# The norms' per-token factor moved behind the weight products, and x times norm weight split tile by tile

## The reference

```python
def rmsnorm(x, g):
    xf = x.astype(F32)
    y = xf * lax.rsqrt(jnp.mean(xf * xf, axis=-1, keepdims=True) + EPS)
    return (y * g.astype(F32)).astype(x.dtype)

h = rmsnorm(x, w['norm_mix'][i]);  x = x + mixer(h)
h = rmsnorm(x, w['norm_ffn'][i])
f = (jax.nn.silu(h @ w['ffn_w_gate'][i]) * (h @ w['ffn_w_up'][i])) @ w['ffn_w_down'][i];  x = x + f
```

## Time and profile before

| | |
|---|---|
| median of three runs | 1917.39 us (1916.46 to 1919.80) |
| the profiled execution | 1914.43 us, span 1912.6 us, mean granted TensorE clock 0.978 |
| PE busy | 1816.6 us (95%), 13287 matmuls |
| PE weight load busy | 1751.6 us (92%) |
| POOL busy | 849.4 us (44%) |
| ACT busy | 619.5 us (32%) |
| DVE busy | 592.2 us (31%) |
| DMA | 153.23 MB, mean 80 GB/s |

### The profile page before, as it was taken

How to read it: one execution, slowest core, us unless ns; L and a number is a source line. 1 busy time by engine, 2 the same in 40 slices (tenths; PEclk the granted TensorE clock), 3 DMA queues, 4 the chain that set the end, 5 groups by cost and what they waited for, 6 DMA issues and landing times.

```text
span 1912.6 us, 33665 instructions
## 1 busy us (share of the span) xinstructions
PE 1816.6 (95%) x13287; PEld 1751.6 (92%) x13287; DVE 592.2 (31%) x887; ACT 619.5 (32%) x846; POOL 849.4 (44%) x1061
## 2 busy tenths in 40 slices
PE   6998999997999999999999999999988999999997
PEld 4898989886999999999999999999977999999996
DVE  2545454555211111000453355344534111111002
ACT  3625252523222222113333333424334222222112
POOL 2544444444454544446443344334424445444443
PEclk9999999997999999999999999999988999999998
DMA  5113121211222222223231343134321222322221
GB/s 149 45 34 79 43 78 44 79 34 46 66 81 82 82 79 83 80 83 103 73 117 58 114 128 112 59 117 119 106 64 58 78 87 77 88 77 83 80 83 57
DMA packets 254284, 153.23 MB, mean 80 GB/s; under 512 B 5136, under 2 KB 246549, under 8 KB 254240
## 3 DMA queue, kind: packets, MB, share of 16 engines
q1 hardware_dynamic: 239726, 140.05, 25.4%
q10 hardware_dynamic: 14514, 12.59, 2.0%
HBM read 138.26 MB, written 14.36 MB: 80 GB/s over the span
## 4 chain that ended last, share of the span: by engine, by line
PE 49%; issue 15%; POOL 10%; DVE 3%; ACT 1%; DMA 0%; POOLq 0%; ACTq 0%; DVEq 0%
PE acc L465 40%; POOL w_lo L457 9%; PE acc L485 7%; PE mx L1511 1%; DVE n_xf L587 1%; PE mx L883 1%; PE mx L528 0%; POOL n_ss L565 0%; POOL xn_lo L571 0%; DVE yT L587 0%; DMA out<-y_out 0%; DVE xn_lo L571 0%; POOL kdm L980 0%; DVE y_out L1506 0%; PE mx L524 0%
## 5 line engine op out<-in xcount | busy, mean ns | idle before, releaser
L457 POOL TENSOR_TENSOR w_lo<-raw,w_hi 128x256 fp32r<-128x256 f32 x932 | 712.7, 797 | 941.5 <-ACT w_hi L449 941.5
L465 PE MATMUL acc<-xn_hi,w_hi 128*128 128x288 f32 x2224 | 498.1, 306 | 2.4 <-ACT kb L721 1.3
L465 PE MATMUL acc<-xn_hi,w_lo 128*128 128x288 f32 x2224 | 477.6, 296 | 0.0
L465 PE MATMUL acc<-xn_lo,w_hi 128*128 128x288 f32 x2224 | 476.8, 296 | 0.0
L449 ACT ACTIVATE w_hi<-raw 128x1024 fp32r<-128x1024 f32 (+1 forms) x237 | 247.0, 1043 | 528.9 <-PE acc L465 528.2
L465 PEld LDWEIGHTS acc<-xn_hi,w_hi 128*128 128x128 f32 x2224 | 358.6, 190 | 15.7 <-issue 7.9
L465 PEld LDWEIGHTS acc<-xn_lo,w_hi 128*128 128x128 f32 x2224 | 359.2, 189 | 0.0
L465 PEld LDWEIGHTS acc<-xn_hi,w_lo 128*128 128x128 f32 x2224 | 358.9, 189 | 0.0
L601 DVE TENSOR_TENSOR x<-acc,x 128x576 f32<-128x576 f32 (+1 forms) x112 | 84.7, 756 | 323.1 <-PE acc L465 321.4
L693 DVE TENSOR_TENSOR f_h<-acc,f_g 128x576 f32<-128x576 f32 x44 | 33.3, 758 | 443.8 <-PE acc L465 443.8
L465 PE MATMUL acc<-h_hi,w_hi 128*128 128x288 f32 x704 | 150.9, 295 | 0.0
(11 more groups left out here) (326 smaller groups left out, 2134.8 us busy)
## 6 DMA issues: line engine op xcount, KB each, us to landing
raw<-in_odd_w_in SPq DMA_DIRECT2D x48, 512.0 KB, 3.7
raw<-in_ffn_w_gate SPq DMA_DIRECT2D x44, 512.0 KB, 3.7
raw<-in_ffn_w_up SPq DMA_DIRECT2D x44, 512.0 KB, 3.7
raw<-in_ffn_w_down SPq DMA_DIRECT2D x32, 512.0 KB, 3.7
raw<-in_even_w_in SPq DMA_DIRECT2D x29, 512.0 KB, 4.0
r_s<-in_state_ret SPq DMA_DIRECT2D x8, 1024.0 KB, 5.5
...
```

The lines of the kernel that those rows point to most:

```text
L457: ins = nc.gpsimd.tensor_tensor(w_lo[:, d, piece], raw[:, s, piece], w_hi[:, d, piece].bitcast(F32), ALU.subtract)
L465: ins = nc.tensor.matmul(out, w, mv[:, tokens], start=first and n == 0, stop=last and n == 2)
```

## The change

For norms 1, 2 and 3 the factor n_rs no longer goes into the moving operand. As a tile of x is finished, ACT squares it and rounds x times norm weight into xn_hi (`square_and_scale`), and DVE forms the remainder in one instruction (`late_low`), between its additions to x. Norms 0 and 4 stay as they were. PE starts the first two units of the next part on these tiles: slices 0 to 5 of both, then `norm_sum`, then slices 6 and 7 of both (`late_units`). POOL now adds seven squares in every norm from 1 on.

The factor is applied where products leave the accumulators. In the feed-forward part DVE multiplies the gate product with n_rs (f_g), ACT applies Silu in place, DVE multiplies f_g with n_rs again, and with the second accumulator. In the odd mixer DVE empties values and gates with n_rs as factor, and ACT applies Silu to the gates afterwards, in place; for q and k the rotary tables `co` are multiplied with n_rs once.

Three further moves: the rows of the convolution states are transposed and copied within the last even head, and SP sends them; the waits for outgoing DMAs ahead of the feed-forward loops go from ACT to DVE; and `rows_unit` begins its first slice when the operand's first half is there (`yl0`, `yal`) and waits for the second half at its second slice. f_h is gone (h_lo takes its place) and zi, xi share the memory of n_sq.

```diff
-O_ACT = ("kdt", "v0", "v1", "ot", "osq", "oln", "oinv", "yh0", "yh1")
+O_ACT = ("kdt", "v0", "v1", "gs0", "ot", "gs1", "osq", "oln", "oinv", "yh0", "yh1")
...
+        def late_units(pe, norm, one, other):
+            for a, b in ((0, KT - 2), (KT - 2, KT)):
+                for phase, j in (one, other):
+                    unit(pe, phase, 0, j, a, b, wait_late=norm)
+                if a == 0:
+                    norm_sum(pe, norm)
...
+                    if mb == 0 and k == 1 and low_1:
+                        low_1()
...
-        POOLED = (0, 5, 7, 5, 7)
+        POOLED = (0, 7, 7, 7, 7)
...
+        def gain(k, t):
+            return cols[:, COL_NORM[k] + t:COL_NORM[k] + t + 1]
+        def square_and_scale(act, k, t):
+            square(act, k, t)
+            nc.scalar.activation(xn_hi[:, t, :], x[:, t, :], ACT.Copy, scale=gain(k, t)).then_inc(q_hi, 1)
+        def late_low(dve, k, t):
+            dve.wait_ge(q_hi, k * KT + t + 1)
+            nc.vector.scalar_tensor_tensor(out=xn_lo[:, t, :], in0=x[:, t, :], scalar=gain(k, t),
+                                           in1=xn_hi[:, t, :].bitcast(F32), op0=ALU.mult,
+                                           op1=ALU.subtract).then_inc(q_low, 1)
...
-            with pe.Fori(0, FT // 2) as i:
-                for t in range(2):
-                    unit(pe, up, i, 2 * t, wait_norm=k if t == 0 else None)
-                    unit(pe, up, i, 2 * t + 1)
+            late_units(pe, k, (up, 0), (up, 1))
+            for j in (2, 3):
+                unit(pe, up, 0, j)
+            with pe.Fori(1, FT // 2) as i:
+                for j in range(4):
+                    unit(pe, up, i, j)
             pe.wait_ge(f_lo, (layer + 1) * FT - 1)
             with pe.Fori(0, KT // 2) as i:
...
-                    act.wait_ge(multiplied, plan.summed(up, i, 2 * t))
-                    act.wait_ge(drained[1], plan.drained(up, i, 2 * t + 1))
-                    nc.scalar.activation(f_g[:, :], pair_view(0), ACT.Silu).then_inc(drained[0], 1)
+                    act.wait_ge(drained[0], plan.drained(up, i, 2 * t) + 1)
+                    nc.scalar.activation(f_g[:, :], f_g[:, :], ACT.Silu).then_inc(f_act, 1)
...
+                    dve.wait_ge(multiplied, plan.summed(up, i, 2 * t))
+                    nc.vector.tensor_tensor(f_g[:, :], pair_view(0), n_rs[:, :], ALU.mult).then_inc(drained[0], 1)
+                    dve.wait_ge(f_act, 2 * n - 1)
+                    nc.vector.tensor_tensor(f_g[:, :], f_g[:, :], n_rs[:, :], ALU.mult).then_inc(f_act, 1)
+                    dve.wait_ge(f_act, 2 * n)
                     dve.wait_ge(multiplied, plan.summed(up, i, 2 * t + 1))
-                    dve.wait_ge(drained[0], plan.drained(up, i, 2 * t) + 1)
-                    nc.vector.tensor_tensor(f_h[:, :], pair_view(1), f_g[:, :], ALU.mult).then_inc(drained[1], 1)
+                    value = ff_tile(h_lo, i, t)
+                    nc.vector.tensor_tensor(value.bitcast(F32), pair_view(1), f_g[:, :], ALU.mult)\
...
+            late = norm_next < 4
+            with dve.Fori(0, KT // 2 - 1 if late else KT // 2) as i:
                 for t in range(2):
                     add_to_x(dve, down, i, t, ds(i * 2 + t, 1))
+            if late:
+                for t in range(KT - 2):
+                    late_low(dve, norm_next, t)
+                for t in range(2):
+                    add_to_x(dve, down, KT // 2 - 1, t, KT - 2 + t)
+                    late_low(dve, norm_next, KT - 2 + t)
...
+            def activate_gate(d):
+                emptied(act, phase, i, 2 + d)
+                o_act.done(nc.scalar.activation(gs[:, d, :], gs[:, d, :], ACT.Silu), f"gs{d}")
...
-            evac(3, gs[:, 1, :], ACT.Silu)
+            activate_gate(1)
             load_table(LN_EXP)
             o_dve.wait(act, h, "cen")
             o_act.done(nc.scalar.activation(osq[:, :, :], of[:, :, :], ACT.Square), "osq")
...
+            dve.wait_ge(q_rs, 3)
+            for n in range(2):
+                ins = nc.vector.tensor_tensor(co[:, n, :], co[:, n, :], n_rs[:, :], ALU.mult)
+            ins.then_inc(s_co, 1)
...
+            def values(j):
+                p = plan.pair(phase, j)
+                dve.wait_ge(multiplied, plan.summed(phase, i, j))
+                nc.vector.tensor_tensor(va[:, j, 0:TP], pair_view(p)[:, 0:TP], n_rs[:, 0:TP], ALU.mult)
+                nc.vector.tensor_tensor(spread(va[:, j, TP:]), pairs(pair_view(p)[:, TP:T]), pairs(n_rs[:, TP:T]),
+                                        ALU.mult).then_inc(drained[p], 1)
+            def gate_in(d):
+                p = plan.pair(phase, 2 + d)
+                dve.wait_ge(multiplied, plan.summed(phase, i, 2 + d))
+                nc.vector.tensor_tensor(gs[:, d, :], pair_view(p), n_rs[:, :], ALU.mult).then_inc(drained[p], 1)
...
             step(ins, "cen")
+            gate_in(1)
             o_act.wait(dve, h, "osq")
             step(nc.vector.tensor_tensor(both[:, :], osq[:, 0, :], osq[:, 1, :], ALU.add), "sq_both")
...
                 add_to_x(dve, phase, i, PLAIN[phase] + m, m)
+                if last and m >= 2:
+                    late_low(dve, 3, m - 2)
...
-            o_dve.wait(pe, h, "yl1")
+            o_dve.wait(pe, h, "yl0")
             for j in range(2):
-                rows_unit(pe, phase, i, PLAIN[phase] + j, PLAIN[phase] + 4 * j, oyh, oyl)
+                rows_unit(pe, phase, i, PLAIN[phase] + j, PLAIN[phase] + 4 * j, oyh, oyl,
+                          low_1=(lambda: o_dve.wait(pe, h, "yl1")) if j == 0 else None)
...
+            for n in range(4):
+                sp.wait_ge(rows_copied, n + 1)
+                k = 2 if n == 0 else 3
...
-            squares_while_splitting(act, split_hi, square, 1, EVEN_END)
-            norm_scalar(act, 1)
-            for n in range(4):
...
+            squares_while_splitting(act, split_hi, square_and_scale, 1, EVEN_END)
+            norm_scalar(act, 1, late=True)
             ffn_scalar(act, 0)
...
+                if last and m:
+                    late_low(dve, 1, m - 1)
+            if last:
+                late_low(dve, 1, KT - 1)
...
+            if last:
+                emptied(pe, phase, i, 3)
+                emptied(pe, phase, i, 4)
+                for t in range(4):
+                    ins = nc.tensor.transpose(acc[0:18, 0, 0, t * P:(t + 1) * P], out_a[:, t, :], ident)
+                ins.then_inc(rows_turned, 1)
...
-            e_dve.wait(pe, h, "ybl")
+            e_dve.wait(pe, h, "yal")
+            if last:
+                pe.wait_ge(rows_copied, 4)
+            e_act.wait(pe, h, "yah")
             for j in range(2):
-                rows_unit(pe, phase, i, PLAIN[phase] + j, PLAIN[phase] + 4 * j, yh, yl)
+                rows_unit(pe, phase, i, PLAIN[phase] + j, PLAIN[phase] + 4 * j, yh, yl,
...
-            pe.wait_ge(rows_copied, 4)
-            norm_sum(pe, 1)
             ffn_tensor(pe, 0)
-            norm_sum(pe, 2)
-            two_units(pe, 2, ("odd_kq", 0), ("odd_kq", 1))
+            late_units(pe, 2, ("odd_kq", 0), ("odd_kq", 1))
             with pe.Fori(0, RET_H - 1) as i:
```

131 lines of the change are left out of this document (59 added, 72 removed).

## The result

Changed kernel 1912.98 us median (20 runs, 1908.85 to 1921.78); kernel before beside it 1917.36 us (20 runs, 1913.82 to 1922.48). Ratio 0.9980, 95% interval 0.9970 to 0.9989. It is faster, as forecast, but by 4 us and not by 9.6. A later comparison of the same two gave 1912.27 against 1917.99, ratio 0.9967 (0.9950 to 0.9984). I take 4.4 to 5.7 us as the gain.

The account below looks back on a forecast made before the run. PE was taken to bound the kernel, other engines counting only where PE waits. 4 + 7.8 + 1 + 1.6 - 4.8 = 9.6 us off gave 1904.8, or 1908 on the median's footing; own range 1900 to 1913, with neighbours 1895 to 1917.

Parts of the forecast that it names:

- Boundary 2: Down phase into the odd mixer: U(0) starts at 919.9, before at 928.59; gain 8.7 less 0.9, so 7.8 us.
- the slow stretch: PE at a lowered clock after a gap; 0.9 us taken off at the second boundary for a possible one.
- the rule of blocked ports: Two-SBUF-input VectorE and SBUF-reading GpSimd instructions block each other wholly; some 3 to 5 us less gain in all.
- Odd heads: Second gate's detour over DVE delays unit 5's split: PE waits 1.3, 0.6 returns; net loss 0.7 us, seven heads 4.8.
- Boundary 3: Last odd head into the second up phase: unit 2 at 1474.3, gain 4.75, slow stretches about 3.7; gain 1 us.
- Boundary 1: Last even head into the first up phase: unit 2 at 484.8 for 492.7, 7.9 us less 4 for clock; gain 4.
- Even heads: Output groups start on the first half while PE would wait for yl; three heads win 1.6 us.
- Up and down loops: Feed-forward loops: two more DVE products per pair of units and Silu 0.85 us later, costed at nothing.
- the rival of 1936 us: Up-phase loops: DVE's second f_g product stretches POOL's split, weight 0.7 us late in 40 places, 28 us; chance 0.08.
- gain eaten by the split chain: Unit 5's wait costs 1.6 us or more a head, late_low blocked at boundaries 1 and 3: 1917 us; chance 0.17.
- the full gain of 21 us: Rival: gaps too short or well placed to lower the clock, odd heads cost little; 1896 us, chance 0.2.

Follow-up runs that it names:

- u0_early: Changed kernel with ScalarE splitting U(0)'s weights before it waits for the norm's sum, not behind the inverse root: 1909.96 us against 1917.99 for the kernel before.
- gate_late: Changed kernel with the odd heads' second-gate Silu and table load moved behind the squares and U(5)'s weight split: 1901.92 us against 1917.99 for the kernel before.
- both_lows: Changed kernel with the output groups waiting for both rounding residues again, in even and odd heads: 1913.14 us against 1917.94 for the kernel before.

## Why the prediction was wrong

The direction and the places were right, and the time lies in the range. The size was not: 4.4 to 5.7 us for 9.6. By its own steps:

*Boundary 2: the step that failed most, 5.3 us measured for 7.8.* What failed is the price of POOL's splits beside DVE's new instructions, put at the price of an undisturbed split, and the size of the slow stretch. The text has "n_rs at 915.6, then ACT splits the first head's weight (1.05) and POOL (2.8): 919.8", and from there 8.7 less 0.9. The chain was right and ran as written:

```profile
919.55 0.69 ACT L575 ACTIVATE n_rs<-n_rs 128x576 f32<-128x576 f32 x1
920.14 1.05 ACT L446 ACTIVATE w_hi<-raw 128x1024 fp32r<-128x1024 f32 x1
```

```profile
921.27 3.65 POOL L454 TENSOR_TENSOR w_lo<-raw,w_hi 128x256 fp32r<-128x256 f32 x4 [9.58 <-ACT w_hi L446]
```

Three sizes in it were off. POOL's split took 3.65 us and not 2.80, as DVE multiplied beside it (how, stands under the rule of blocked ports): U(0) began 18.1 us after the down phase's end, for 17.4. That end itself came 1.1 us later, counted from down0's first addition, than before (PE's first slice of the key unit at 906.96, its norm sum before at 902.50, and 3.4 us of offset). DVE's late_low now runs beside POOL there, and PE waits 0.33 and 0.22 us for w_lo, which it didn't; its matmuls shift by the whole 1.1 us at these two stops. The 16 pieces of w_lo in 880:907 have a mean of 938 ns,

```profile
L454 POOL TENSOR_TENSOR w_lo<-raw,w_hi 128x256 fp32r<-128x256 f32 x16 | 14.5, 938 | 2.3 <-ACT w_hi L446 2.3
```

against 739 of 17 in the like stretch before. I had counted that the down phase gives ACT and DVE 17 us a tile and forgot what their work does to POOL's. And the slow stretch behind the gap took 1.7 us, not 0.9 (from U(0)'s start to the first product of rotated queries and keys 8.01 us for 6.34). Together 8.7 - 0.7 - 1.1 - 1.7 = 5.2, measured 5.3. What I should have said is that a split put behind the inverse root is free to move ahead of it: u0_early shows 4.1 us at that one place.

*Odd heads.* "Net 0.7 us, in seven heads: 4.8 us": measured 0.88, 6.2 us. The mechanism was right. In the frame of the head, PE's variance product came 0.17 us later, which I had put at nothing; from there to the kvs product it took 9.68 us for 8.29, that is 1.39 more where I had 1.3 (the row at 1037.31 shows 1.06 of it as a wait); and 0.7 came back at the output groups, for 0.6. gate_late confirms the cause: 0.77 of the 0.88 us goes with the order alone. In the last head PE's wait for the sum of squares grew by 1.5 us (4.08 to 5.57) and that at the output groups fell by 0.8 (3.62 to 2.82), both as forecast.

*Boundary 3.* 1.0 forecast with the last odd head, 0.0 measured. In the heads' frame, which is 4.3 us later than before, unit 0 began at 1452.1, where I had 1452.3. Unit 1 began at 1460.8 for 1460.0: POOL's two splits ahead took 3.30 and 3.28 us for 2.80, and its three additions spanned 5.5 us for 4.3, all with late_lows beside them. Unit 2 began at 1477.2 for 1474.3, 1.9 us earlier than before where I had 4.75. The rest of that difference is a low clock behind unit 1's wait, 1.7 us, and a wait that was 0.5 longer:

```profile
1465.10:1471.10 6.00, 6.00 (x34) 6.00 (x35) 0.00 (x0) 0.00 (x0) 0.00 (x0) 0.72 0.29 87
1481.40:1487.40 6.00, 5.98 (x31) 5.98 (x32) 0.00 (x0) 0.00 (x0) 2.72 (x4) 0.66 0.60 173
```

Behind unit 2 the clock took the remaining 1.9. In all it cost 3.6 us, for 3.7 forecast; the term that failed is mainly POOL's price again.

*Boundary 1.* 4.0 forecast with the last even head. A mark ahead of the early start shows both parts at once, the first copy of oT in that head. Before and after:

```profile
437.17 0.23 DVE L1416 COPY oT<-mx 128x64 f32<-128x64 f32 x1 [2.12 <-PE mx L1511]
```

```profile
444.56 0.23 DVE L1468 COPY oT<-mx 128x64 f32<-128x64 f32 x1 [0.76 <-PE mx L1568]
```

From here to down0's first addition it is 342.45 us before and 338.43 after: 4.0 us won, as forecast (338.5 and 337.0 in the changed kernel's other profiles, 342.3 to 344.6 in those of the kernel before). On this footing unit 0 began at 464.3 for 464.7, unit 1 at 471.7 for 470.5, unit 2 at 486.4 for 484.8, and the two slow stretches cost 1.7 and 2.4 us, for the 4 taken off. The clock differs in that head too: from the copy to the first output addition PE had 0.50 before and 0.83 after, so a part of the 4.0 may be luck.

*Even heads.* 1.6 forecast for three of them, and that much of PE's waiting is gone (both_lows above). The times say 1 to 3 us with the last one, by subtraction, under a scatter of up to 12 us between single executions.

With these footings the terms are 4.0 + 5.3 + 0.0 + 1.6 - 6.2 = 4.7 us, for 4 + 7.8 + 1 + 1.6 - 4.8 = 9.6, and 4.4 to 5.7 at the medians. Of the 4.9 us that are missing boundary 2 has 2.5, the odd heads 1.4 and boundary 3 1.0.

*Up and down loops.* Nothing, as forecast: the rival of 1936 us fell. DVE's second product runs beside none of POOL's pieces in the 44 places, so the case against that rival was right.

*The rule of blocked ports.* The 24 late_lows take 807 ns at the least, 926 in the median and 1403 at the most:

```profile
L564 DVE SCALAR_TENSOR_TENSOR xn_lo<-x,cols,xn_hi x24: 807/926/1403, 458.2 to 1461.9; 128x576 fp32r<-128x576 f32 x24
```

What decides is which of the two engines began first. Here it is POOL, and below it DVE:

```profile
1450.60 1.76 POOL L589 TENSOR_TENSOR n_ss<-n_ss,n_sq 128x576 f32<-128x576 f32 x1
1451.67 1.31 DVE L564 SCALAR_TENSOR_TENSOR xn_lo<-x,cols,xn_hi 128x576 fp32r<-128x576 f32 x1
```

```profile
886.06 0.85 DVE L564 SCALAR_TENSOR_TENSOR xn_lo<-x,cols,xn_hi 128x576 fp32r<-128x576 f32 x1 [4.55 <-ACT xn_hi L559]
886.24 1.26 POOL L454 TENSOR_TENSOR w_lo<-raw,w_hi 128x256 fp32r<-128x256 f32 x1
```

The late_low ends 0.62 us behind POOL's addition (1452.98 and 1452.36), the split's piece 0.59 us behind the late_low (887.50 and 886.91). So it is everywhere in this trace: of the 22 late_lows that start while a POOL instruction runs, 18 end 0.61 to 0.62 us behind it, whatever was left of it; three met only its last 0.1 us and took 819 ns; the longest, 1403 ns, stood behind the piece of w_lo after it too. But for that one, a piece of w_lo that starts within a late_low ends 0.58 to 0.60 us behind it. The delay shows as a longer instruction, not as idle time before it. By the Trainium skill (SBUF — State Buffer, Summary: rules for kernel authors) the second of two such instructions waits until the first has finished, and the trace agrees. The text had weighed that rule, with 3 to 5 us less gain, and left it out of the sum. In U(0)'s split the first piece, begun at 921.27, takes 1.08 us and ends 0.58 us behind DVE's product with `co` (921.02, 0.75 us long). I had written 0.82 to 1.3 for DVE, which held but for that one, and 2.80 for POOL, which didn't: the contention was booked on one side only. No run keeps late_low and POOL apart, so what it cost at each boundary rests on the traces and not on an experiment.

What the text did not ask is whether the split waits that it listed had to be there. It had one at each boundary, and its rival "gain eaten by the split chain" named them, but all its cases kept the splits where they stood, the full gain of 21 us too. Waits for split weights rose from 5.5 us to 27.7, and moving those of the up phases alone took the changed kernel from 1912.3 to 1890.7 us.
